# Second mixer of a float32 transformer chain: the 16 meta columns padded to a full block of 128, and the values product one step later

## The reference, cut to what matters

```
q, k, v = split(h @ w_qkv, 3)             # 8 heads, 2 halves of 64 for q and k, v is 128 wide
for i, t in two blocks of 128 queries:
    logits = q_half @ k_half.T + bias     # 128 x 272 for each head and half
    p      = softmax(logits)              # over the 272 keys
    a      = p[half 0] - lam * p[half 1]
    o      = a @ v                        # 128x272 times 272x128
o = rmsnorm(o, subln_g) * (1 - lambda_init);  out = o @ w_o
```

## Time and profile before

| what | value |
|---|---|
| median of three runs (lowest, highest) | 1469.21 us (1467.02, 1470.15) |
| span of the profiled execution, first to last instruction | 1470.1 us; the page lists no other time of it |
| PE busy | 1449.7 us, 99% of the span |
| DVE, ACT, POOL busy | 941.3, 665.4, 53.6 us |
| mean granted TensorE clock | 0.995 |
| attention of the second mixer | from about 861 to 909 us of the span |

### The profile page before, as it was taken

The page is one execution under the profiler, slowest core; times in us unless marked ns, Lnnn a source line. Parts: engine busy times, 40 slices in busy tenths (PEclk is TensorE's granted clock), DMA queues, the critical chain, the costliest instruction groups (busy, mean ns, idle before and its releaser), DMA issues.

```text
span 1470.1 us, 26580 instructions
## 1 busy us (share of the span) xinstructions
PE 1449.7 (99%) x11144; PEld 1387.9 (94%) x11144; DVE 941.3 (64%) x1209; ACT 665.4 (45%) x891; POOL 53.6 (4%) x72
## 2 busy tenths in 40 slices
PE   9999999999999999999999999999999999999998
PEld 9999999978999999999999977899999997999887
DVE  6666568556765566766557665776566865677653
ACT  5444346445534435444335356544444444534432
POOL 0000010010000000000010000100001010100000
PEclk9999999999999999999999999999999998999999
DMA  6586755511455675555455520465656550356552
GB/s 213 174 222 186 216 192 164 170 35 59 150 181 179 170 212 173 172 173 180 148 183 175 173 86 2 129 214 174 187 176 193 175 164 7 115 158 200 199 181 107
DMA packets 238906, 234.02 MB, mean 159 GB/s; under 512 B 29791, under 2 KB 233492, under 8 KB 238816
## 3 DMA queue, kind: packets, MB, share of 16 engines
q1 hardware_dynamic: 238024, 232.33, 50.6%
q10 hardware_dynamic: 792, 0.40, 0.1%
HBM read 231.52 MB, written 1.12 MB: 158 GB/s over the span
## 4 chain that ended last, share of the span: by engine, by line
PE 92%; DVE 3%; ACT 2%; DMA 1%; issue 1%; POOL 1%; POOLq 0%; DVEq 0%; SPq 0%; ACTq 0%
PE acc L627 22%; PE acc L626 22%; PE acc L628 22%; PE acc L689 4%; PE aux L924 2%; PE aux L856 2%; PE aux L855 2%; PE aux L854 2%; PE acc L695 2%; PE aux L627 1%; PE aux L628 1%; PE aux L626 1%; PE acc L1182 1%; PE aux L1096 1%; PE acc L1219 1%
## 5 line engine op out<-in xcount | busy, mean ns | idle before, releaser
L626 PE MATMUL acc<-x_hi,w_hi 128*128 128x272 f32 (+1 forms) x1960 | 560.9, 286 | 4.1 <-DVE z L1918 3.4
L627 PE MATMUL acc<-x_lo,w_hi 128*128 128x272 f32 (+1 forms) x1960 | 560.8, 286 | 0.0
L628 PE MATMUL acc<-x_hi,w_lo 128*128 128x272 f32 (+1 forms) x1960 | 558.9, 285 | 0.0
L1783 DVE TENSOR_TENSOR w_lo<-raw,w_hi 128x2048 fp32r<-128x2048 f32 (+1 forms) x229 | 482.9, 2113 | 115.6 <-ACT w_hi L1349 115.3
L1349 ACT ACTIVATE w_hi<-raw 128x2048 fp32r<-128x2048 f32 (+3 forms) x251 | 406.9, 1627 | 163.9 <-DMA raw<-in_ffn_w_down 47.9
L626 PEld LDWEIGHTS acc<-x_hi,w_hi 128*128 128x128 f32 x1960 | 370.3, 189 | 6.9 <-DVE z L1918 3.8
L627 PEld LDWEIGHTS acc<-x_lo,w_hi 128*128 128x128 f32 x1960 | 369.0, 188 | 0.4 <-issue 0.2
L628 PEld LDWEIGHTS acc<-x_hi,w_lo 128*128 128x128 f32 x1960 | 369.3, 188 | 0.0
L626 PE MATMUL acc<-hid_hi,w_hi 128*128 128x272 f32 (+1 forms) x704 | 202.8, 288 | 0.0
L627 PE MATMUL acc<-hid_lo,w_hi 128*128 128x272 f32 (+1 forms) x704 | 201.7, 287 | 0.0
L628 PE MATMUL acc<-hid_hi,w_lo 128*128 128x272 f32 (+1 forms) x704 | 200.9, 285 | 0.0
(11 more groups left out here) (331 smaller groups left out, 1737.9 us busy)
## 6 DMA issues: line engine op xcount, KB each, us to landing
raw<-in_ffn_w_gate SPq DMA_DIRECT2D x44, 1024.0 KB, 5.3
raw<-in_ffn_w_up SPq DMA_DIRECT2D x44, 1024.0 KB, 5.4
raw<-in_ffn_w_down SPq DMA_DIRECT2D x32, 768.0 KB, 4.4
raw<-in_ffn_w_down SPq DMA_DIRECT2D x32, 640.0 KB, 4.2
raw<-in_w_up SPq DMA_DIRECT2D x16, 1024.0 KB, 5.5
raw<-in_w_down SPq DMA_DIRECT2D x16, 1024.0 KB, 4.8
raw<-in_na_w_qkv SPq DMA_DIRECT2D x12, 1024.0 KB, 5.2
raw<-in_da_w_qkv SPq DMA_DIRECT2D x12, 1024.0 KB, 5.2
```

The source lines that it names most:

```text
L626: nc.tensor.matmul(o, wh, xh, start=first, stop=False)
L627: nc.tensor.matmul(o, wh, xl, start=False, stop=False)
L628: return nc.tensor.matmul(o, wl, xh, start=False, stop=last)
L1783: nc.vector.tensor_tensor(w_lo[:, slot, w], raw[:, slot, w], w_hi[:, slot, w].bitcast(F32), ALU.subtract)\
```

## The change

- The third block of the mixture's columns is padded: `da_mix` is 384 columns wide, and columns 272 to 383 are set to zero once by POOL (semaphore `mix_padded`). The mixture still writes 272.
- `v_meta` has 128 rows; POOL sets it to zero once before ACT writes its 16 rows (semaphore `values_padded`).
- PE turns three blocks of 128 columns and multiplies three blocks of 128 rows.
- DVE copies 384 columns of the turned blocks in one instruction; ACT's copy of the meta block and its semaphore are gone.
- PE's values product comes four steps after the scores instead of three, so there is one step more (0 to 19). `keep_warm` has no product in steps 4 to 15 and none in steps 18 and 19; it keeps 6 in steps 2, 3, 16 and 17.

```
-        da_mix = sb("da_mix", [P, 2, NT], F32, c)
+        da_mix = sb("da_mix", [P, 2, 3 * P], F32, c)
-        v_meta = sb("v_meta", [NM, D], F32, c)
+        v_meta = sb("v_meta", [P, D], F32, c)
...
-                for step in range(16 + 3):
-                    if step == 3:
+                for step in range(16 + 4):
+                    if step == 4:
                         pe.wait_ge(acc_free, PHASES[2 * DA].a0 + 12)
                     if 2 <= step < 16:
                         pe.wait_ge(s["logits"], 2 * step)
-                        keep_warm(aux[:, 0, 3 * P:], 6 if step < 4 else 1 - step % 2)
+                        if step < 4:
+                            keep_warm(aux[:, 0, 3 * P:], 6)
                         da_scores(step)
-                    if step >= 16:
+                    if 16 <= step < 18:
                         pe.wait_ge(s["logits"], 32)
                         keep_warm(aux[:, 0, 3 * P:], 6)
-                    if step >= 3:
-                        idx = step - 3
+                    if step >= 4:
+                        idx = step - 4
...
                         pe.wait_ge(s["turned_copied"], idx + 1)
-                        pe.wait_ge(s["turned_rest"], idx + 1)
                         wait(pe, s["evicted"], idx - 3)
-                        for b in range(2):
-                            nc.tensor.matmul(o, da_turned[:, idx % 2, P * b:P * b + P], v_rows[:, b, v0:v0 + P],
-                                             start=b == 0, stop=False)
-                        nc.tensor.matmul(o, da_turned[0:NM, idx % 2, 2 * P:3 * P], v_meta[:, v0:v0 + P],
-                                         start=False, stop=True).then_inc(s["pv"], 1)
+                        for b in range(3):
+                            values_ = v_rows[:, b, v0:v0 + P] if b < 2 else v_meta[:, v0:v0 + P]
+                            mm = nc.tensor.matmul(o, da_turned[:, idx % 2, P * b:P * b + P], values_,
+                                                  start=b == 0, stop=b == 2)
+                        mm.then_inc(s["pv"], 1)
                     if 2 <= step < 18:
                         idx = step - 2
                         if idx == 0:
                             pe.wait_ge(s["v_copied_act"], 2)
+                            pe.wait_ge(mix_padded, 1)
                         pe.wait_ge(s["mixed"], idx + 1)
                         wait(pe, s["turned_copied"], idx - 1)
-                        wait(pe, s["turned_rest"], idx - 1)
                         bank = aux[:, 2 + idx % 2, :]
-                        for b in range(2):
-                            nc.tensor.transpose(bank[:, P * b:P * b + P], da_mix[:, idx % 2, P * b:P * b + P], ident[:, :])
-                        nc.tensor.transpose(bank[0:NM, 2 * P:3 * P], da_mix[:, idx % 2, NX:NT], ident[:, :])\
-                            .then_inc(s["turned"], 1)
+                        for b in range(3):
+                            tr = nc.tensor.transpose(bank[:, P * b:P * b + P], da_mix[:, idx % 2, P * b:P * b + P], ident[:, :])
+                        tr.then_inc(s["turned"], 1)
...
-                    if 2 <= step < 18:
-                        idx = step - 2
-                        act.wait_ge(s["turned_copied"], idx + 1)
-                        wait(act, s["pv"], idx - 1)
-                        nc.scalar.activation(da_turned[0:NM, idx % 2, 2 * P:3 * P], aux[0:NM, 2 + idx % 2, 2 * P:3 * P],
-                                             ACT.Copy).then_inc(s["turned_rest"], 1)
...
-                        nc.vector.tensor_copy(da_turned[:, idx % 2, 0:2 * P], aux[:, 2 + idx % 2, 0:2 * P])\
+                        nc.vector.tensor_copy(da_turned[:, idx % 2, :], aux[:, 2 + idx % 2, 0:3 * P])\
                             .then_inc(s["turned_copied"], 1)
...
+                if k == DA:
+                    pool.wait_ge(sum_ready, 2 * DA)
+                    nc.gpsimd.memset(v_meta[:, :], 0.0).then_inc(values_padded, 1)
+                    pool.wait_ge(panel_used, PHASES[2 * DA].p0 + 12)
+                    nc.gpsimd.memset(da_mix[:, :, NT:], 0.0).then_inc(mix_padded, 1)
```

More of the change, by code:

```diff
@@ L371, in program @@
             names += {NA: ["proj", "vm_turned", "vm_copied"],
-                      DA: ["vm_turned", "vm_copied", "turned_rest", "stats", "weighted", "mixed", "sd"], MIX: []}[k]
+                      DA: ["vm_turned", "vm_copied", "stats", "weighted", "mixed", "sd"], MIX: []}[k]
             mixers[k] = {n: sem(f"{tag}_{n}") for n in names}
+        values_padded = sem("values_padded")
+        mix_padded = sem("mix_padded")
         meta_scores = sem("meta_scores")
@@ L552, in value_blocks_in @@
                     g, b = divmod(hd, 8)
-                    sp.dma_start(v_blocks[NM * b:NM * b + NM, g, 64 * b:64 * b + 64], v_meta[:, 64 * hd:64 * hd + 64])\
+                    sp.dma_start(v_blocks[NM * b:NM * b + NM, g, 64 * b:64 * b + 64], v_meta[0:NM, 64 * hd:64 * hd + 64])\
                         .then_inc(blocks_full, 16)
@@ L1597, in values @@
                     act.wait_ge(s["vm_turned"], 1)
-                    nc.scalar.activation(v_meta[:, :].rearrange("p (a n) -> p a n", a=2), aux[0:NM, 0:2, :],
+                    if k == DA:
+                        act.wait_ge(values_padded, 1)
+                    nc.scalar.activation(v_meta[0:NM, :].rearrange("p (a n) -> p a n", a=2), aux[0:NM, 0:2, :],
                                          ACT.Copy).then_inc(s["vm_copied"], 1)
@@ L2168, in mix @@
                     nc.vector.scalar_tensor_tensor(
-                        out=da_mix[:, idx % 2, :], in0=da_probs[:, (u + 1) % 4, :], scalar=row_recip[:, u + 1:u + 2],
+                        out=da_mix[:, idx % 2, 0:NT], in0=da_probs[:, (u + 1) % 4, :], scalar=row_recip[:, u + 1:u + 2],
                         in1=da_probs[:, u % 4, :], op0=ALU.mult, op1=ALU.add).then_inc(s["mixed"], 1)
```

## The result

| what | before | changed |
|---|---|---|
| median of 15 runs each (lowest to highest), us | 1469.13 (1466.23 to 1482.3) | 1460.72 (1458.22 to 1468.9) |
| span of the profiled execution, us | 1470.1 | 1459.2 |
| mean granted TensorE clock in it | 0.995 | 0.997 |
| one step, turning of item 2 to turning of item 13, over 11 | 2.44 | 1.88 |
| scores of step 3 to the first turned head | 42.05 | 33.45 |

The ratio is 0.9943, interval 0.9927 to 0.9959: 8.4 us less by the medians. A second series with 12 runs of the changed kernel gave 1461.05 us and 0.9941 (0.992 to 0.9961).

What follows compares the result with a forecast made beforehand. PE's order of work bounds the kernel, the attention being a ring of small operations with no engine full. Gains 1.06 + 5.98 + 1.7 = 8.7 us; 1469.2 - 8.7 = 1460.5 us, eight in ten between 1457.0 and 1464.8.

Steps and rivals of the forecast that it cites:

- Padded product: PE's values product: three gaps around the 16-row records shrink to 0.11 each, 0.29 us less a step.
- Padded turning: PE's turning of the third block, 128 columns of weights instead of 16: cost 0, at most 0.05 us a step.
- One copy: DVE's copy grows from 256 to 384 columns, 0.13 us more; ACT's copy and hop, 0.30, leave the chain.
- The step: Attention step: 1.90 us, from a PE-DVE chain of 3.77 over two steps; the later product removes the wait for the copy.
- Start: Attention's first steps, up to the turning of item 2: it comes 1.06 us earlier.
- Middle: Turning of item 2 to that of item 13: 11 steps at 1.90 instead of 2.44, gain 5.98 us.
- End: From the turning of item 13 to ACT's table load: 5.55 us instead of 7.28, gain 1.7.
- POOL and added waits: POOL's memsets of v_meta and da_mix: cost 0 under cover; if the cover were gone, 0.4 us once.
- Rival A: Values product: gaps are not from the row count and padding buys nothing; step 2.15, 1464.2 us, chance 0.12.
- Rival B: Attention: DVE becomes the bound through dearer copy and hops; step 2.10, 1462.7 us, chance 0.2.
- Rival C: Attention: granted clock falls without small products; 10 us at low level costs 5 us (1465.5), chance 0.06, slower 0.02.
- Rival D: Third mixer: its low-clock stretch is missed or doubled, widening to 1456.5 to 1465.5; off by over 2 us, chance 0.15.

Runs made afterwards that it cites:

- e1_narrow: Changed kernel with the third part of the values product again 16 rows, turning and copy still padded; 1465.71 us (kernel before 1471.25).
- e6_wide_copy: Changed kernel with DVE's copy of the turned blocks widened from 384 to 512 columns; 1459.14 us (kernel before 1469.06).
- e5_mix_first: Changed kernel with DVE making the mixture ahead of the copy of the turned blocks; 1463.03 us (kernel before 1469.06).
- e2_lag3: Changed kernel with the values product back at three steps after the scores; 1462.54 us (kernel before 1471.25).
- e8_two_copies: Changed kernel with the product three steps after the scores and ACT copying the 128-row third block behind DVE's copy; 1462.42 us (kernel before 1469.06).
- e3_lag4_only: Kernel before with the product four steps after the scores and small products as changed, nothing padded, two copies; 1465.52 us (kernel before 1471.25).
- e4_pad_only: Kernel before with padding and one copy only, product three steps after the scores, small products as before; 1463.50 us (kernel before 1471.25).
- e7: Changed kernel without the small products of steps 3, 16 and 17; 1454.75 us, ratio to the kernel before 0.989.
- e9: Changed kernel without small products in steps 3, 16, 17, ACT's table load in step 16, 4 small products instead of 10 behind the attention; 1456.16 us, ratio 0.9898.
- e11: Changed kernel without the 6 small products of step 3, nothing else; 1458.87 us (kernel before 1468.09).

## Why the prediction was right

The time, 1460.5 us, was met within 0.3. The mechanism of most parts held; one attribution did not.

1. *Padded product.* Said 0.29 us a step, measured 0.31 (e1_narrow against the changed kernel). The gaps do come from the change of row count.
2. *Padded turning.* Said to be free; the passage from the first turning record to the scores is 0.42 and 0.48 in turns, the longer one where the scores wait for the logits, and no cost shows.
3. *One copy.* Said 0.55, measured 0.55 to 0.56.
4. *The step.* Said 1.90 by a chain of 3.77 over two steps; measured 1.88 and 3.76, and e6_wide_copy shows that this chain is the bound. PE alone is 1.85 by its rows (0.42 + 0.65 + 0.78), said 1.83. DVE alone was said to be 1.81 and is 1.80 by its rows; e5_mix_first, where it is the bound, bears that out (1.80 + 0.12, measured 1.91). The three bounds lie within 0.08 of each other, the chain last, as the forecast had them. **The step that failed is the sentence "the product of item s-4 finds its copy done in the step before, so the wait goes".** The wait goes, but that step isn't needed for it: the single copy takes it away as well; e2_lag3, without the later step, has the same stretch. In e8_two_copies, with neither, the second copy costs 0.20 a step and 3.7 us in all; so the hand-over was a real cost, and either edit should remove it. That the later step does so with padding and two copies wasn't run; e3_lag4_only points to it, with the step of e1_narrow. The small products were to go "too", at no price or gain of their own; e4_pad_only shows that keeping them costs 2.40 us. And of what the earlier trace rows shows as the wait, 0.36 of 0.5 a time is left in the changed kernel's view; on PE's timeline of the kernel before, the product comes 0.93 after the scores in one step and 0.71 in the other, where PE alone needs 0.66.
5. *Start.* Said 1.06, measured 0.98 (scores of step 3 to turning of item 2: 4.19, now 3.21).
6. *Middle.* Said 5.98, measured 6.21 (26.88 less 20.67).
7. *End.* Said 1.7, measured 1.42 (turning 13 to table load: 7.28, now 5.86). The small records of step 16 wait for the last logits and start 0.48 after the turning instead of 0.33, and from the first of the twelve to the next product are 1.44 instead of 1.32.
8. *POOL and added waits.* Both memsets are there, and nobody waits for them:

```profile
781.52 0.95 POOL L2577 MEMSET v_meta<- 128x1024 f32 x1 [14.64 <-PE aux L917]
861.34 0.29 POOL L2579 MEMSET da_mix<- 128x224 f32 x1 [78.87 <-PE acc L630]
```

The sum is 8.61 us against 8.7 (0.98 + 6.21 + 1.42); that it agrees more closely than its parts is luck, since the middle was 0.23 more than forecast and start and end 0.36 less. Another 0.37 was gained ahead of the scores of step 3, 0.31 of it already at the scores of step 2, ahead of all that was changed on PE (862.85, now 862.54; its cause wasn't followed). The sentence that the gain "stays to the end" was right only by the medians: in the profiled pair 2.7 were given back and 3.9 came in the third mixer. That the time was met within 0.3 is in part luck, then: what lies behind the attention moves single runs by several us.

Rival A fell by e1_narrow; its own step was priced too low, 2.12 where 2.19 is measured. Rival B fell for the changed kernel (no hop was dearer), with 0.08 of room a step for DVE: e5_mix_first uses it up. Rival C didn't happen in the changed kernel (1.00 throughout its attention); e7 and e9 show that it can, and e11 that it need not, with the same edit in step 3. It did lose 1.7 us to a low clock behind its attention, which no rival had. Rival D happened in the profiled execution. It also sets the spread: runs of the changed kernel with a mean granted clock of 0.998 took 1459.43, 1458.84 and 1458.22 us, those with 0.991 and less 1468.9 and 1467.01.

## What to carry to other kernels

In a ring of short operations, a block with few rows can cost PE more than a full one at its changes of row count (0.31 us a step here), and padding it with zeros can be cheaper than leaving work out. Two edits that can remove the same wait don't add up: take each back alone before crediting it, and look at what filled the gap before, since it turns from free into a cost. When a stage has become shorter, read on behind it, landmark by landmark, for what the earlier start now meets.

## What the runs showed of the hardware

- Two float32 matmul records of 16 rows between records of 128 rows cost 0.31 us a step more than two of 128 rows, for an eighth of the rows.
- A DVE operation that reads what the short one ahead of it wrote started 0.25 us after that one's start (e5_mix_first), one that doesn't 0.13 (e6_wide_copy, in the steps where it doesn't wait for PE). I had priced both alike.
- The busy time of an engine whose records overlap can read as full while it still waits: DVE shows 5.97 of 6.00 us where its own work is 1.80 of the 1.88 a step.
- POOL's two-input addition of 128x256 took 0.74 us by itself (e7, e9) and 2.65 beside DVE's two-input operation on a panel. The Trainium skill, "GPSIMD Engine Reference", Key points, has POOL share its SBUF interfaces with VectorE, with contention when DVE reads two inputs from SBUF; the traces agree, and the size is the ratio of these two numbers, 3.6.
